# Two layer blocks on one core: a chunked recurrence with its near-block inverses, loads and gate steps reordered, and a depthwise convolution with two tiles on TensorE

## The reference

```python
def step(state, inp):
    r_t, w_t, k_t, v_t, a_t, b_t = inp
    sa = jnp.einsum('bhvk,bhk->bhv', state, a_t)
    state = (state * w_t[:, :, None, :] + sa[..., None] * b_t[:, :, None, :]
             + v_t[..., None] * k_t[:, :, None, :])
    return state, jnp.einsum('bhvk,bhk->bhv', state, r_t)
...
y = wkv7_scan(rh, decay, kh, vh, -kk, kk * ah)      # then a group norm per head, weights, a bonus
return (y * g) @ w_o, v_first                        # g = sigmoid(xg @ g1) @ g2
```

```python
u = ua * jax.nn.sigmoid(ub)
u = causal_depthwise_conv(u, conv_w, conv_b)         # CONV_KERNEL = 31
u = jax.nn.silu(layer_norm(u, conv_norm_g, conv_norm_b))
y_a = u @ w_conv_out
```

## Time and profile before

| | |
|---|---|
| Median of 3 runs | 1154.82 us (1154.34 to 1154.87) |
| Profiled execution, its own time | 1157.31 us |
| Its span, first to last instruction | 1155.3 us |
| Mean granted clock of TensorE | 0.982 |
| TensorE matmuls busy | 1099.9 us (95%) |
| VectorE busy | 830.5 us (72%) |
| ScalarE busy | 561.2 us (49%) |
| GpSimd busy | 44.2 us (4%) |
| HBM read | 202.33 MB |

### The profile page before, as it was taken

One profiled execution on the slowest core, in us unless ns is written; L12 is line 12 of the kernel. 1 busy time (PEld: TensorE's weight loads), 2 busy tenths in 40 slices (PEclk: granted clock), 3 DMA queues, 4 the chain that ended last, 5 costly groups with the idle time before them and its releaser, 6 DMA issues.

```text
span 1155.3 us, 18315 instructions
## 1 busy us (share of the span) xinstructions
PE 1099.9 (95%) x7268; PEld 919.2 (80%) x7268; DVE 830.5 (72%) x1176; ACT 561.2 (49%) x718; POOL 44.2 (4%) x50
## 2 busy tenths in 40 slices
PE   9999999999999746799999999999999999999998
PEld 7887888889778526777888888798888788999996
DVE  4654554558398874778999987999999976555554
ACT  6545543345565223454433446456476756444443
POOL 0000000000001050100111100000000000000000
PEclk9999999999999877999999999999999999999999
DMA  9585555643233202277999974455440364555542
GB/s 330 186 260 182 183 172 190 211 158 122 93 131 111 49 27 58 81 271 262 362 327 339 333 247 146 138 181 182 148 154 37 128 201 146 182 167 196 187 140 109
DMA packets 138315, 205.83 MB, mean 178 GB/s; under 512 B 19768, under 2 KB 95821, under 8 KB 138254
## 3 DMA queue, kind: packets, MB, share of 16 engines
q1 hardware_dynamic: 130820, 177.63, 46.8%
q0 software_dynamic: 6560, 25.19, 5.9%
q10 hardware_dynamic: 874, 2.15, 0.5%
HBM read 202.33 MB, written 1.57 MB: 177 GB/s over the span
## 4 chain that ended last, share of the span: by engine, by line
PE 82%; DVE 11%; issue 3%; ACT 2%; DMA 2%; ACTq 0%; DVEq 0%
PE ps L747 24%; PE ps L749 24%; PE ps L748 24%; DVE wide L3296 2%; DVE wl L2546 2%; PE ps L973 1%; DMA raw<-in_ab_w_in 1%; PE ps L1191 1%; PE ps L824 1%; PE ps L1106 1%; PE ps L1299 1%; PE ps L1462 1%; DVE wh_plain L3034 1%; PE ps L1105 1%; PE ps L1130 1%
## 5 line engine op out<-in xcount | busy, mean ns | idle before, releaser
L2546 DVE TENSOR_TENSOR wl<-raw,wh 128x2048 fp32r<-128x2048 f32 (+2 forms) x154 | 345.5, 2249 | 98.7 <-ACT wh L1753 98.4
L747 PE MATMUL ps<-wh,xh 128*128 128x512 f32 (+3 forms) x856 | 339.4, 397 | 2.6 <-DVE wl L2546 1.4
L749 PE MATMUL ps<-wl,xh 128*128 128x512 f32 (+3 forms) x856 | 332.6, 389 | 0.0
L748 PE MATMUL ps<-wh,xl 128*128 128x512 f32 (+3 forms) x856 | 332.4, 388 | 0.0
L1753 ACT ACTIVATE wh<-raw 128x2048 fp32r<-128x2048 f32 (+2 forms) x154 | 286.9, 1878 | 53.0 <-PE ps L749 33.1
L747 PEld LDWEIGHTS ps<-wh,xh 128*128 128x128 f32 x856 | 161.5, 189 | 39.4 <-issue 2.1
L749 PEld LDWEIGHTS ps<-wl,xh 128*128 128x128 f32 x856 | 161.5, 189 | 35.2
L748 PEld LDWEIGHTS ps<-wh,xl 128*128 128x128 f32 x856 | 161.8, 189 | 33.6 <-issue 1.0
L747 PE MATMUL ps<-wh,gh 128*128 128x512 f32 x288 | 114.0, 396 | 0.8 <-DVE wl L2546 0.8
L749 PE MATMUL ps<-wl,gh 128*128 128x512 f32 x288 | 113.7, 395 | 0.0
L748 PE MATMUL ps<-wh,gl 128*128 128x512 f32 x288 | 113.6, 394 | 0.0
(11 more groups left out here) (448 smaller groups left out, 1327.0 us busy)
## 6 DMA issues: line engine op xcount, KB each, us to landing
wide<-in_w_ada POOLq DMA_DIRECT2D x24, 1024.0 KB, 10.2
raw<-in_ffn_w_gate SPq DMA_DIRECT2D x44, 512.0 KB, 4.7
raw<-in_ffn_w_up SPq DMA_DIRECT2D x44, 512.0 KB, 5.7
raw<-in_ffn_w_down SPq DMA_DIRECT2D x22, 1024.0 KB, 5.2
raw<-in_w_mlp_in SPq DMA_DIRECT2D x16, 1024.0 KB, 7.1
raw<-in_w_mlp_out SPq DMA_DIRECT2D x16, 1024.0 KB, 5.0
raw<-in_w_in SPq DMA_DIRECT2D x16, 512.0 KB, 4.9
raw<-in_w_in SPq DMA_DIRECT2D x8, 1024.0 KB, 5.1
```

The costliest lines, as they stand in the source:

```text
L747: pe.matmul(o, lh, rh, start=start, stop=False)
L748: pe.matmul(o, ll, rh, start=False, stop=False)
L749: return pe.matmul(o, lh, rl, start=False, stop=stop)
L2546: v.tensor_tensor(wl[:, s, 0:width], raw[:, s, 0:width], f32(wh[:, s, 0:width]), ALU.subtract).then_inc(lo_ready[s], 1)
```

## The change

- SyncE loads the second `w_o` block whole behind the first, and `a_columns` of group 0 stands before `near_in(0)`, that of group 1 behind it.
- The near blocks of a half lie side by side: one store for a half instead of two, one load, and three loads of `near_c` instead of eight. `near_blocks` reduces in two parts.
- `near(1)` stands before `y1_out(0)` on VectorE instead of behind `y1_out(1)`; its products go to `W(8)` and no longer to `wh_plain`.
- The gate products of half 0 stand behind `gram_v(1)`, ahead of the flips of groups 2 and 3; those of half 1 behind `gram_ts(3)`. The flips wait for `gate_out`.
- GpSimd does the bonus products and additions of both halves first, then waits for `near(0)`, then does the gate steps of both.
- ScalarE splits the first `w_o` block behind `ar_out(1)` and the second behind `bk_out(3)`.
- The convolution's tiles 6 and 7 go to TensorE as four 64x64 products per tap; tile 7's halves lie swapped in PSUM, so its vectors and the last rows of `w_conv_out` are loaded swapped (three DMAs for those blocks instead of one). VectorE makes the diagonals, one instruction for four taps; ScalarE brings the tiles out in four copies.

The core of the diff (semaphore tables and buffer names left out):

```diff
 (SyncE, recurrence_loads)
                 in_place(("o",) + O_ORDER[0])
+                in_place(("o",) + O_ORDER[1])
+                a_columns((0,))
                 near_in(0)
-                a_columns((0, 1))
+                a_columns((1,))
                 near_out(0)
                 near_in(1)
-                in_pieces(("o",) + O_ORDER[1], 0, (0, 1))
                 near_out(1)
-                in_pieces(("o",) + O_ORDER[1], 0, (2, 3))
...
+                sp.dma_start(dst[:, 0:8, :], src[:, 0:8, :]).then_inc(S("inverse"), 16)
+                for half in range(2):
+                    a, b = 64 * half, 64 - 64 * half
+                    sp.dma_start(dst[a:a + 64, 8:16, :], src[b:b + 64, 8:16, :]).then_inc(S("inverse"), 16)
 (GpSimd, between the additions and the gate steps)
+            pool.wait_ge(S("wkv.near"), B("wkv.near") + 1)
 (TensorE)
-                    pe.wait_ge(S("wkv.gkvc"), B("wkv.gkvc") + g - 1)
+                    pe.wait_ge(S("gate_out"), B("gate_out") + g - 1)
...
-            gate_product(0, 0, 2)
-            gate_product(0, 1, 6)
+                gate_product(g // 2, 0, 2)
+                gate_product(g // 2, 1, 6)
...
+                for d, k in zip(diags[i % 2], taps):
+                    for swapped in range(CONV_PE):
+                        for r in range(2):
+                            rows, o = slice(64 * r, 64 * r + 64), 64 * (r ^ swapped)
+                            m = pe.matmul(ps[o:o + 64, CONV_BANK(r), SEQ:2 * SEQ], d[rows, 64 * swapped:64 * swapped + 64],
+                                          upad[rows, KT - CONV_PE + swapped, k:k + SEQ], start=k == 0, stop=k == CK - 1)
 (ScalarE)
             ar_out(1)
+            split_in_place(("o",) + O_ORDER[0])
             gkv_out(0)
             gkv_out(1)
+            gate_out(0, 0)
+            gate_out(0, 1)
             for g in (2, 3):
                 ar_out(g)
                 bk_out(g)
-            gate_out(0, 0)
-            gate_out(0, 1)
+            split_in_place(("o",) + O_ORDER[1])
+            gate_out(1, 0)
+            gate_out(1, 1)
...
-                if g == 0:
-                    act.wait_ge(S("wkv.near"), B("wkv.near") + 2)
-                    split_in_place(("o",) + O_ORDER[1])
 (VectorE)
             for g in (0, 2):
-                if g == 2:
+                if g == 0:
+                    near(1)
+                else:
                     carry(0, 1)
...
+            def diag_taps(i):
+
+                if i >= 2:
+                    v.wait_ge(S("conv_mm"), B("conv_mm") + i - 1)
+                else:
+                    v.wait_ge(S("ro_T"), B("ro_T") + 3)
+                k0, n = i * TAP_BATCH, min(TAP_BATCH, CK - i * TAP_BATCH)
+                w = cols[:, CONVW + (KT - CONV_PE) * CK:CONVW + KT * CK].rearrange("p (a k) -> p k a", a=CONV_PE)[:, k0:k0 + n, :]
+                v.tensor_tensor(DIAG_BATCH(W, i, n), unit.unsqueeze(1).unsqueeze(1).to_broadcast([P, n, CONV_PE, CH]),
+                                w.unsqueeze(3).to_broadcast([P, n, CONV_PE, CH]), ALU.mult).then_inc(S("diag"), 1)
...
+            diag_taps(0)
             for i in range(0, NH, 2):
                 scored(i)
-                conv(3)
+                diag_taps(i + 1)
+                conv(2)
                 finish(i)
                 conv(1)
                 scored(i + 1)
+                if i + 2 < NH:
+                    diag_taps(i + 2)
```

More of the change, by code:

```diff
@@ L300, in make_plan @@
             for k in range(2):
-                p.block((w, n, k))
+                p.block((w, n, k), dmas=3 if (w, k) == ("conv_out", 1) else 1)
     for k in range(2):
@@ L468, in sources @@
                          flat.rearrange("p (a n) -> p a n", a=2))]
+            if what == "conv_out" and name[2]:
+                v, o = flat.rearrange("p (a n) -> p a n", a=4), name[1] * 512
+                last = [(SRC[what][D - 128 + 64 * (1 - half):D - 64 * half, o:o + 512], v[64 * half:64 * half + 64, 3, :]) for half in range(2)]
+                return [(kblock(SRC[what], o, 512, 1)[:, 0:3, :], v[:, 0:3, :])] + last
             if name == ("ab_in", IN_ORDER[0], 0):
@@ L2445, in _ @@
             act.wait_ge(S("conv_mm"), B("conv_mm") + NH)
-            for kt in range(KT - CONV_PE, KT):
-                act.activation(W3(2, KT)[:, kt, :], CONV_OUT(ps, kt), ACT.Identity, bias=col("conv_b_2", kt)).then_inc(S("conv_pe"), 1)
+            for half in range(2):
+                for r in range(2):
+                    rows, kt = slice(64 * half, 64 * half + 64), KT - CONV_PE + (r ^ half)
+                    m = act.activation(W3(2, KT)[rows, kt, :], ps[rows, CONV_BANK(r), SEQ:2 * SEQ], ACT.Identity,
+                                       bias=cols[rows, ROWS["conv_b_2"] + kt:ROWS["conv_b_2"] + kt + 1])
+                m.then_inc(S("conv_pe"), 1)
             split(("attn_out", 1, 1))
@@ L2987, in near_blocks @@
                 link(m)
-                v.tensor_reduce(tmps[g]["far"].rearrange("p (u c) -> p u c", u=8), tmps[g]["xt"].rearrange("p (u b c) -> p u c b", u=8, b=4),
-                                AX_X, ALU.add).then_inc(S("wkv.nc"), 1)
+                rows = NEAR_ROWS(W, g // 2).rearrange("p (y g u c) -> p y g u c", y=2, g=2, u=4)
+                for y in range(2):
+                    m = v.tensor_reduce(rows[:, y, g % 2], tmps[g]["xt"][:, 256 * y:256 * y + 256].rearrange("p (u b c) -> p u c b", u=4, b=4), AX_X, ALU.add)
+                m.then_inc(S("wkv.nc"), 1)
             def mask_b(g):
@@ L3043, in inverse_out @@
             def inverse_out(g):
[L3045 removed]
+                v.wait_ge(S("inverse"), B("inverse") + 48 * (g // 2 + 1))
                 if g >= 2:
                     v.wait_ge(S("wkv.r1"), B("wkv.r1") + g - 1)
[L3048 to L3052 removed]
+                shape = [P, 4, 4, 16]
+                blocks = near_c[:, :].rearrange("p (y g u c) -> p y g u c", y=2, g=2, u=4)
+                for y in range(2):
+                    m = v.tensor_tensor(tmps[g]["t8"][:, 256 * y:256 * y + 256].rearrange("p (u b c) -> p u b c", u=4, b=4),
+                                        blocks[:, y, g % 2].unsqueeze(2).to_broadcast(shape),
+                                        masks[:, MI["near"]:MI["near"] + CH].rearrange("p (b c) -> p b c", b=4).unsqueeze(1).to_broadcast(shape), ALU.mult)
+                m.then_inc(S("wkv.t8"), 1)
             def one_more(sem, b, dst, done):
```

128 lines of the change are left out of this document (45 added, 83 removed).

## The result

The changed kernel takes 1129.63 us (median of 4 runs, 1127.59 to 1130.05) against 1154.84 for the kernel before (1154.34 to 1156.58): ratio 0.9776 [0.9759, 0.9793], 25.2 us faster. The forecast was 1126.6 in 1120 to 1136. The profiled execution took 1129.51 us, span 1127.5, where the working expected 1129.1: by spans (first to last instruction) 27.8 us came back, against a sum of 28.2.

What follows compares the result with a forecast made beforehand. TensorE sets the time, idling 23.90 us before off_2 through ScalarE's queue order and the near(1) chain. Recurrence 26.3 plus convolution 1.9 gives 28.2 us: 1157.31 to 1129.1 profiled, less 2.5 for median 1126.6, range 1120 to 1136.

Steps and rivals of the forecast that it cites:

- (a): Recurrence: second output block loaded behind the first and split after the second groups' copies removes ScalarE's wait; cost nothing.
- (b): Recurrence: paired stores merged into one land in 3.3 us (bounds 2.2, 6.2); near(0) starts at 385.3.
- (c): Recurrence: first gate products ahead of second flips, 2.2 us each; flips at 388.2, second groups' blocks from 393.1 to 401.4.
- the bounds of nothing and 2 us: Recurrence: GpSimd's early steps beside near_blocks and masks, taken to cost nothing; without the skill's rule it could be 2 us.
- (d): Recurrence, VectorE: near(1) ahead of y1_out(0) starts at 402.6, takes 9.0 us (between 6.56 and 13.47), ends at 411.6.
- (e): Recurrence, after near(1): VectorE's copies end at 415.8, off_2(0) starts at 415.9 instead of 440.55, 24.6 us.
- the 1.7 us of warmth: Recurrence, TensorE: the two off_2 products run at the high clock, 1.7 us more gained.
- The convolution: Second block: attention loop 2.0 us longer, the 2.11 us hole before conv_mean closes; sum -1.9 us, bounds +2 and -5.
- The 1.7 us counted for the clock: Second block: over the 7 us after the hole before conv_mean the clock, at 0.76, stays up; 1.7 us gained.
- The rival that the quadrants do not overlap: Convolution taps: quadrants run one after another, 31 taps cost 42.8 us more, time 1171; chance 0.03.
- The sum: Whole kernel: 26.3 us from the recurrence plus 1.9 from the convolution, 28.2; profiled execution from 1157.31 to 1129.1.

Runs made afterwards that it cites:

- early block alone: Kernel before with only the second output block loaded whole behind the first, split behind bk_out(3), and near products in another buffer; 1143.10 us, ratio 0.9885.
- recurrence part alone: Kernel before with only the changes to loads, stores, near, gate products, GpSimd order and ScalarE splits, old convolution kept; 1130.80 us, ratio 0.9779.
- convolution part: Kernel before with only the new convolution (quadrant taps, VectorE diagonals, loop order, copies, swapped loads), old recurrence kept; 1154.97 us, ratio 0.9990.
- longer hold: Changed kernel with GpSimd's second-half gate steps also waiting until y1_out of groups 0 and 1 is done; 1129.24 us, ratio 0.9760.
- without the hold: Changed kernel without GpSimd's wait for near(0) before the gate steps; 1129.64 us, ratio 0.9783.
- late split: Changed kernel with ScalarE's third output block split moved from ahead of r2_out(2) to behind r4_out(3); 1126.96 us, rerun 1125.96 beside the changed kernel's 1130.78.
- hold until r4 alone: Changed kernel with GpSimd's second-half gate steps also waiting for VectorE's r4 copies of groups 0 and 1; 1129.40 us, ratio 0.9779.

## Why the prediction was right, and what it missed

- **What bounds it.** Right: queue order on ScalarE and a contended `near(1)` in front of it. The early block alone took 11.7 us off `off_2(0)`, less contention in `near(1)` 6.2, its place 4.1, its earlier begin 2.7.
- **(a) The early block at no cost.** Right: the splits stand at 375.43 and 393.31 without a wait, and SyncE was past `a_columns` before the store of 379.35.
- **(b) Merged stores.** 3.1 us to landing against 3.3. `near(0)` began at 384.47 (385.3 forecast) and took 6.56 us (6.6).
- **(c) Gate products and flips.** 2.2 each, flips at 387.68 (388.2), blocks at 392.93 (393.1), masks to 401.2 (401.4). GpSimd's four early steps (376.23 to 380.7) cost nothing: the steps on PSUM beside them took what they had taken, L2980 0.67 us against 0.68. Nor did its first gate steps beside the second groups' masks: 8.27 us with GpSimd busy 3.17 of them, against 8.08 with none, and 0.17 of the difference are the reduces in two parts. That decides between the bounds of nothing and 2 us.
By the Trainium skill (SBUF — State Buffer, Who interferes with whom) a VectorE instruction with at most one SBUF input, outside the two-port modes, does not contend with GpSimd; the masks agree. The copies of 1.23 and 1.20 us with the early block alone have one SBUF input too and were slowed. The same section counts copies among the instructions that can run in such a mode; whether these did, no run here shows.
- **(d) `near(1)`.** 402.54 to 411.51, 8.97 us against 402.6, 411.6 and 9.0, and the middle value was right for its reason, since without GpSimd it took 6.5.
- **(e) `off_2(0)`.** 415.88 against 415.9, with some luck. 0.46 us of it lay ahead of the change already (the grams began at 374.40 instead of 374.86; in the second profile of the changed kernel they began at 374.84 and `off_2(0)` at 416.35). And what came last was TensorE: `off_1` could begin only behind `y1_out(0)`, at 412.25, and ran at the low clock (1.98 and 1.96), while VectorE's copy, which the forecast took as the bound, was over at 415.73. Its two parts ran at 1.74 and 1.05, so 1.2 of the 1.7 us of warmth came. The first scores moved from 854.65 to 828.51: 26.1 us against 26.3.
- **The convolution.** The loop grew 2.06 us (35.03 to 37.09, 2.0 forecast), `conv_mean` came 0.2 earlier relative to the scores (0.3), the hole closed and the clock stayed up: 1.8 against 1.9. The 1.7 us counted for the clock cannot be counted on: in the recurrence part alone the hole left the clock at 1.00, and there the new convolution is 0.8 us better. The rival that the quadrants do not overlap is excluded by 1.96 against 4.70 us.
- **The sum.** 27.8 us between the profiled executions against 28.2.
- **Where it missed: the step to the median.** The working said that the profiled execution "lay 2.5 us above the median of 1154.82, so the median becomes **1126.6**". That took the 2.5 us for something outside the changed parts that both kernels carry. The runs point elsewhere. The forecast read 1.68 us as a gate part at the low clock; the three parts behind it took 2.07 to 2.08, so the low clock cost this execution more than that row told. Two executions of the old recurrence differ by 3.5 us at `off_2(0)` (440.55 and 437.02) with the gate products at the low clock in the one and at the high one in the other, and by 3.6 at the first scores (854.65 and 851.08). With the early block alone they ran at the low clock too, and that execution was 1.8 us above its median, where the convolution part's was 1.5 below. The 38 executions of the kernel before whose mean clock is on record agree: the 16 at 0.983 or more have a median of 1153.6 us, the 22 below it 1156.4, and the profiled one, at 0.982 and 1157.31, is one of the latter kind. The change removes just this stretch: its gate products ran at the high clock in both of its profiles (1.10 to 1.13 a part). So a median execution should gain near 28.2 - 2.5 = 25.7, which gives 1129.1. That is an estimate: how the 2.5 us divide over the stretches of a median execution no trace shows. Over all runs shown, the kernel before has a median of 1155.2 us (42 runs, 1151.97 to 1158.75) and the changed one 1130.05 (9 runs, 1127.59 to 1132.37).

**The changed kernel has such a stretch too.** Its second profiled execution took 1132.37 us, with `off_2(0)` at 416.35, 0.5 later. By the product L1372 it was 2.1 later (462.58 against 460.48). Of the 1.6 us between, 1.1 are three waits of TensorE (first profile, then second), and the rest is low clock behind `off_2(2)`:

```profile
430.65 0.39 PE L1193 MATMUL ps<-wide,xh_plain 64*64 64x64 f32 x10 [0.35 <-issue]
434.26 0.39 PE L1193 MATMUL ps<-raw 64*64 64x64 f32 x10 [1.05 <-issue]
437.96 0.39 PE L1193 MATMUL ps<-wide 64*64 64x64 f32 x11 [0.52 <-issue]
```

```profile
431.76 0.39 PE L1193 MATMUL ps<-wide,xh_plain 64*64 64x64 f32 x10 [0.90 <-issue]
435.64 0.39 PE L1193 MATMUL ps<-raw 64*64 64x64 f32 x10 [1.33 <-issue]
439.61 0.39 PE L1193 MATMUL ps<-wide 64*64 64x64 f32 x11 [0.80 <-issue]
```

The three waits sum to 1.92 and 3.03 us. With the recurrence part alone and with the longer hold they are 3.03 as well, and each of these three profiled executions was the slowest of its series; without the hold they are 0.50 and with the late split 0.25, and these two were the fastest. (One does not fit: with the hold until r4 alone the waits are gone, and it lay in the middle, with products at the low clock in their place.) The first scores then came at 830.44 in the second profile and at 830.57 with the recurrence part alone, against 828.51, about the 2.0 us by which that part fell short by spans. So single profiles of the changed recurrence differ by some 2 us here, as much as the hold was to bring, and the 4.85 us of the late split's first trace rest on the medians taken side by side, not on the trace.

What stays open: what TensorE waits for there, since the profile names no releaser, and why the clock rises sooner in some executions than in others.

## What to carry to other kernels

An engine's queue order is a dependency: an early job that waits for a DMA belongs behind every copy that another engine waits for, and after one such stall is mended the same pattern should be looked for further on (here the third block, 4.8 us more). When a profiled execution is above the median, find the stretch in which it is slow before the difference is carried over; if the change removes that stretch, the difference goes with it. And a gain of 2 us read from one profile against another is no more than one program's executions differ by. Holding GpSimd's steps tends to move their contention with VectorE: 3.0 us went to `y1_out` and the split, 2.0 to the unpacking of the inverses, 0.5 where they met the splits alone, and nothing where VectorE read PSUM.

## What the runs showed of the hardware

- A VectorE step of 8 columns takes 0.17 us alone and 1.2 us while GpSimd's float32 steps of 512 columns (1.27 us each) run beside it, seven times as long, where a step of 512 columns grows from 0.69 to 1.60. So the order of the small steps against GpSimd's work decides the cost.
- 64x64 products of 256 columns: 32 in 1.96 us when neighbours lie in different quadrants, in 4.70 us when eight neighbours share one; the second is 0.147 us a product where a 128x128 one follows its neighbour by 0.23.
- A store of 128 KB in 64-byte pieces landed in 3.1 us, as one of 64 KB did.
- The same wait of 2.1 us ahead of `conv_mean` stands in an execution of the kernel before with a granted clock of 0.76 over the 7 us around it, and in one of the recurrence part alone with 1.00; the gate products, behind waits of 2.29 and 0.53 us in one and of 2.40 and 0.53 in the other, ran mostly at 2.07 us a part in the one and at 1.12 in the other.
